# RWKV-7 state pass of a two-layer encoder kernel: the score products alternate between the two heads of a pair, and four unused 512-column products per chunk are added

## The reference

```python
def step(S, inp):
    r_t, w_t, k_t, v_t, a_t, b_t = inp
    sa = jnp.einsum('bhvk,bhk->bhv', S, a_t)
    S = S * w_t[:, :, None, :] + sa[..., None] * b_t[:, :, None, :] + v_t[..., None] * k_t[:, :, None, :]
    return S, jnp.einsum('bhvk,bhk->bhv', S, r_t)
_, y = lax.scan(step, jnp.zeros((bsz, H, Dh, Dh), F32), xs)
```

## Time and profile before

| | us |
|---|---|
| median of 3 runs | 1537.95 |
| lowest and highest | 1529.24 and 1540.2 |
| the profiled execution, its time | 1530.25 |
| its span in the trace | 1528.4 |
| TensorE busy in the span | 1319.8 (86%) |
| VectorE busy in the span | 893.7 (58%) |
| first state block, about | 1214 to 1344 |
| second state block, about | 1345 to 1421 |

### The profile page before, as it was taken

How to read it: one execution, slowest core, us unless ns; L and a number is a source line. 1 busy time by engine, 2 the same in 40 slices (tenths; PEclk the granted TensorE clock), 3 DMA queues, 4 the chain that set the end, 5 groups by cost and what they waited for, 6 DMA issues and landing times. The chain is left out here.

```text
span 1528.4 us, 20526 instructions
## 1 busy us (share of the span) xinstructions
PE 1319.8 (86%) x8434; PEld 1103.1 (72%) x8434; DVE 893.7 (58%) x1191; ACT 480.3 (31%) x822; POOL 307.5 (20%) x156
## 2 busy tenths in 40 slices
PE   4999999899779969959997999998334799999698
PEld 4677888678569848858886888885122698889587
DVE  5277754930257664159975665843888758265841
ACT  5233244222346651132421122312553211212310
POOL 2232211211023362032211111221301300000320
PEclk9999999989889979979999999999665557799899
DMA  5212112320300042232331425221000000010523
GB/s 183 43 42 66 31 46 70 96 70 15 138 22 2 2 138 83 96 76 90 99 97 52 121 64 176 52 83 56 0 1 1 1 1 1 2 56 2 193 82 112
DMA packets 117558, 97.79 MB, mean 64 GB/s; under 512 B 37016, under 2 KB 102680, under 8 KB 117336
## 3 DMA queue, kind: packets, MB, share of 16 engines
q1 hardware_dynamic: 103832, 77.45, 17.1%
q10 hardware_dynamic: 13632, 19.01, 3.8%
HBM read 70.23 MB, written 24.51 MB: 62 GB/s over the span
## 5 line engine op out<-in xcount | busy, mean ns | idle before, releaser
L167 PE MATMUL banks<-xt_lo,w_hi 128*128 128x512 f32 x816 | 323.2, 396 | 6.2 <-POOL w_lo L497 6.2
L168 PE MATMUL banks<-xt_hi,w_lo 128*128 128x512 f32 x816 | 319.9, 392 | 0.0
L169 PE MATMUL banks<-xt_hi,w_hi 128*128 128x512 f32 x816 | 319.6, 392 | 0.0
L497 POOL TENSOR_TENSOR w_lo<-features,w_hi 128x1024 fp32r<-128x1024 f32 x55 | 148.9, 2708 | 529.5 <-ACT w_hi L506 529.5
L167 PEld LDWEIGHTS banks<-xt_lo,w_hi 128*128 128x128 f32 x816 | 154.6, 189 | 42.1 <-POOL w_lo L497 6.7
L169 PEld LDWEIGHTS banks<-xt_hi,w_hi 128*128 128x128 f32 x816 | 154.5, 189 | 32.7
L168 PEld LDWEIGHTS banks<-xt_hi,w_lo 128*128 128x128 f32 x816 | 154.5, 189 | 31.2
L550 ACT ACTIVATE temporaries<-banks 128x1024 f32<-128x1024 f32 x47 | 56.1, 1193 | 328.5 <-PE banks L169 319.8
L506 ACT ACTIVATE w_hi<-features 128x1024 fp32r<-128x1024 f32 x55 | 57.8, 1055 | 27.9 <-PE banks L169 26.7
L295 PE MATMUL banks<-temporaries,features 128*128 128x128 f32 x256 | 38.3, 314 | 27.5 <-DVE temporaries L272 27.5
L167 PE MATMUL banks<-xt_lo,oout_mh 128*128 128x512 f32 x128 | 51.1, 399 | 11.9 <-DVE xt_lo L1581 11.9
(11 more groups left out here) (449 smaller groups left out, 2601.2 us busy)
## 6 DMA issues: line engine op xcount, KB each, us to landing
features<-in_even_w_in SPq DMA_DIRECT2D x26, 512.0 KB, 4.0
features<-in_odd_w_in SPq DMA_DIRECT2D x25, 512.0 KB, 4.3
features<-in_x SPq DMA_DIRECT2D x8, 512.0 KB, 8.6
even_gates<-temporaries ACTq DMA_DIRECT2D x8, 512.0 KB, 2.6
features<-even_gates SPq DMA_DIRECT2D x8, 512.0 KB, 8.1
features<-in_even_w_out SPq DMA_DIRECT2D x8, 512.0 KB, 3.5
temporaries<-in_x SPq DMA_DIRECT2D x8, 512.0 KB, 4.6
h_between_layers<-features SPq DMA_DIRECT2D x8, 512.0 KB, 3.1
```

What stands on the lines that cost most here:

```text
L167: nc.tensor.matmul(out, w[0], x[1], start=start, stop=False)
L168: nc.tensor.matmul(out, w[1], x[0], start=False, stop=False)
L169: return nc.tensor.matmul(out, w[0], x[0], start=False, stop=stop)
L497: nc.gpsimd.tensor_tensor(wl[n % 2], wr[n % NW], wh[n % 2].bitcast(F32), ALU.subtract).then_inc(low, 1)
```

## The change

`pairs` now walks over the three products outside and over the two heads inside, so that neighbouring products use opposite row halves of the array and write different banks. It waits once, for both copies of the previous pair. A new helper `unread` multiplies a broadcast column of `hot_r` with `hot_r` repeated to 512 columns, and nothing reads the result. One such product stands in each `turn`, behind its wait and ahead of its transposes (into the bank of the transposes, which they overwrite), and two stand ahead of the wait for SA in step 5 (into the bank of `read`, which R has left). That is four for each chunk and 64 in the kernel.

```diff
     def tensor(pe):
+        def unread(bank):
+            nc.tensor.matmul(co.ps[:, bank, :].rearrange("p (a b) -> p a b", b=32), co.hot_r[:, 0:1].to_broadcast([P, P]),
+                             co.hot_r.rearrange("p (o b) -> p o b", o=1).to_broadcast([P, 16, 32]), start=True, stop=True)
+
         def turn(c, j):
             if c or j:
                 pe.wait_ge(tok_out, 2 * c + j)
+            unread(2)
             for i, src in enumerate((x.b, x.k, x.v)):
                 last = nc.tensor.transpose(turns[:, i * P:(i + 1) * P], src[:, j, c * P:(c + 1) * P], ident)
             last.then_inc(turned, 1)
 
         def pairs(c, j):
             ct = slice(c * P, (c + 1) * P)
-            for a, rows in enumerate(halves):
-                h = 2 * j + a
-                if c or j:
-                    pe.wait_ge(kept, 4 * c + h - 1)
-                for i, (key, query) in enumerate(((x.b, x.r), (x.k, x.kk), (x.k, x.r))):
-                    last = nc.tensor.matmul(scores(h)[:, i * P:(i + 1) * P], key[rows, j, ct], query[rows, j, ct], start=True, stop=True)
-                last.then_inc(pairs_made, 1)
+            if c or j:
+                pe.wait_ge(kept, 4 * c + 2 * j)
+            for i, (key, query) in enumerate(((x.b, x.r), (x.k, x.kk), (x.k, x.r))):
+                for a, rows in enumerate(halves):
+                    last = nc.tensor.matmul(scores(2 * j + a)[:, i * P:(i + 1) * P], key[rows, j, ct], query[rows, j, ct], start=True, stop=True)
+                    if i == 2:
+                        last.then_inc(pairs_made, 1)
...
             yield 10 * c + 6
+            for _ in range(2):
+                unread(3)
             pe.wait_ge(sa_out, c + 1)
```

## The result

| | us |
|---|---|
| median after (4 runs, 1514.38 to 1517.98) | 1517.18 |
| median before (4 runs, 1529.24 to 1540.2) | 1535.38 |
| ratio after to before, with its 95% interval | 0.9899 (0.986 to 0.9938) |
| profiled execution before and after | 1530.25 and 1514.38 |

A second set of runs of the changed kernel gave 1518.69 and a ratio of 0.9917 (0.9882 to 0.9952). The change saves about 1%. The forecast was 1517, with 20.4 us saved; the ratio stands for 15.5 us, and the two profiled executions differ by 15.9. The 52 executions of the kernel before that stand beside the experiments have a median of 1530.5, and against that the saving is 12 to 13 us.

A forecast was written before the change was run, and what follows sets the result against it. TensorE was taken to bound both state blocks, in the first through its 0.50 clock. First block -26.7, clock falls +5, second block +1.3 summed to -20.4 us, giving 1517 us, with 1504 to 1536 to hold 8 times in 10.

The forecast's parts named there:

- Part 1: Scores in each chunk: alternating halves overlap, saving 0.59 us a block at half clock and 0.33 at full.
- Rival C: TensorE in each chunk: alternation brings no overlap, products cost full price, 19 us slower, 1557 us; chance 0.05.
- The joined wait: Ahead of each block of scores: the single wait for both of VectorE's copies costs nothing in sum.
- Part 2: Unused products in each chunk: none hides in waits; four cost 0.87 us at full clock, 1.70 at half.
- Part 3: First state block: clock rises in the first chunk and mostly stays up, 130.0 to 103.3 us, 26.7 us less.
- the sum: State blocks: -26.7 us for the first, +5 for renewed clock falls, +1.3 for the second, -20.4 us in all.
- two falls: First state block: clock falls again where the array is thin; 2.5 us for each of two, 5 us lost.
- My rule, length times clock: First state block: each chunk's length times granted clock gives its work at full clock, 8.2 to 15.4 us.
- A (the clock stays): First state block: TensorE is already occupied, so the clock stays as it is; +4.5 us, 1542 us; chance 0.16.
- B (VectorE takes over): First state block: clock rises but chunks wait for VectorE, half the gain goes; about -10 us, 1528; chance 0.13.

The follow-up runs named there:

- the run with the thin products: Changed kernel, but each unused product contracts over 32 rows instead of 128, with the same 512 columns: 1563.88 us, ratio 1.0217.
- the late ones alone: Alternating scores, with unused products only in the first state block from the fifth chunk's growth on: 1514.2 us, ratio 0.989.

## Why the prediction was right, and where its reasons were not

**Part 1, the overlap of the alternating scores: right.** I took 0.86 us for a block at full clock, and it took 0.87. The saving is 0.32 us a block, shown by the timeline and by the run with the scores alone. At half clock, for which I had 1.58 us, the run with the thin products has 1.58 (L2411 to L2446):

```profile
1240.78 1.65 PE L2411 MATMUL banks<-features 64*128 64x128 f32 x12
1242.36 1.97 PE L2446 MATMUL banks<-temporaries,big 128*128 128x64 f32 x8
```

Rival C is out. The joined wait cost nothing that the second block's chunks show.

**Part 2, the price of a product: a little low.** I took 0.217 us from stretches in which such products follow each other. Between float32 products one costs 0.25 us on average over a chunk (9.7 against 8.7 us with the scores of before, 9.1 against 8.1 with the new ones). So a chunk at full clock became 0.35 us longer (8.74 to 9.09) and not 0.2. At half clock one ahead of the transposes is 0.59 us and two ahead of the growth are 1.00 (1309.87 to 1310.87 in the changed kernel), for the 0.42 each that I took:

```profile
1323.96 0.79 PE L2394 MATMUL banks<-one_hot 128*128 128x512 f32 x1
...
1324.55 0.84 PE L2402 MATMUL banks<-constants,features 128*128 128x128 f32 x3
```

That none of it hides held. With the block's start at 0.50, the second block lost 4.7 us and not 1.3.

**Part 3, the clock: the sign right, the split wrong.** The step that failed is "I expect the clock to rise in the first chunk and mostly stay up", in its second half. For chunks 1 to 5 the sum had 56.3 us against 71.0, and 52.4 came; the clock was up in the first of them and not midway. For chunks 6 to 8 it had 39.2 us plus 5 for "two falls", and they took 15.6, 20.1 and about 18. My rule, length times clock, took these chunks to run at nearly full clock. But the clock falls there again: 33 us at 0.50 in the 63 us from chunk 6 to the second half's first read, where "two falls" at 2.5 us each stood for 10. That term alone is some 10 us too good. What makes the clock fall there isn't shown. The groups of the inverting program are thin, and TensorE waits for copies between them, but the kernel with the products in the first block has two courses in the same chunks, 62.6 us at 0.74 and 54.2 at 0.87.

Term by term, the sum had -0.2 us for the start, -14.7 for chunks 1 to 5, -6.8 for chunks 6 to 8 with the falls, and +1.3 for the second block. The two profiles have -1.2, -18.6, +5.9 (with the start of the second block) and +4.7. That is 9.2 us less for the state blocks, where the forecast had 20.4. The other 6.8 of the 15.9 us lie in code that the change doesn't touch. The time of 1517 was luck in one more way: it was taken from 1537.95, the median of three runs; from the 1530.5 of the 52 later ones the same 20.4 us would have given 1510.

**What the early gain was worth.** It was credited against one course of the kernel before. Its second profile had the same 52 us with no change at all. What the change really does is to shorten the time at the low clock in sum: some 81 us at 0.50 from first to last read became 40, twice, and 184.4 us came of 192 to 194. That is 8 to 10 us, and 1.2 more at the start of the block.

**What the products are for.** I laid the clock to both parts together, and the prediction treated the products as what fills the chunk. The early clock needs neither both nor the products, and in the kernel before it came up once with neither. The second block, where half of them stand, gives nothing for them. If they are worth something in the first block, it is in the middle stretch: 63.3, 62.6 and 54.2 us with them, 66.0 without, 68.7 with the late ones alone. But these are single profiles of kernels whose own courses differ by 8 us, and the medians don't settle it: 1512.96 and 1513.3 with the first block's products, 1516.39 without any, all intervals overlapping. All of the change's measured saving comes with the alternating scores alone.

**The rivals.** A (the clock stays) did not come. Its reading, that an occupied engine is enough, is refuted twice: by the 51 us of the earlier trace rows in the trace of before, and by the thin products, with which TensorE was at least as occupied and the clock lower. The sentence of the Trainium skill's page "TensorE: Matmul & The Clock Gate" (section "What's actually happening") on how busy the PE has been holds here only if busy is not read as occupied. B (VectorE takes over) came in part: chunk 3 is VectorE's, at 11.4 us, and the waits for its copies are the 3.0 and 1.2 us above. That is not half of the gain of chunks 1 to 5, 18.6 us. The state blocks' balance of 9.2 us is near B's 10, but for other reasons: the low clock of the late chunks and the price of the products.

**What stays open.** The medians say 12.7 to 15.5 us, and the traces show 9 to 11 for the state blocks. The times of before reach from 1521.66 to 1543.45 over all sets, and its three profiled executions lie at 1529 to 1532. Their spread goes with the clock: of the 52, the 17 of 1536 us and more have a mean granted clock of 0.889 to 0.900, the eight under 1525 have 0.903 to 0.909. So longer and shorter courses exist that no profile caught; where in the kernel they differ isn't known. The start of the first block moves by some 4 us between executions of the changed kernel, in code that the change doesn't touch. I didn't separate these. Why the clock takes one course or the other in the same program stays open too. That the close fit of 1517 to 1517.18 is owed to errors that cancel is clear from the terms above.

## What to carry to other kernels

Where an engine's clock depends on what it does, one profile is one course of that clock: profile the kernel before a second time before a slow stretch is credited as a gain, and set the time of each profiled execution beside the median: two of the profiles here lay 11 us off it. Products that contract over half the rows should alternate between the halves, into different banks; here it saved a quarter of the block, and alone it gave as short a time as the whole change. Unused products are a price paid at every place where they stand, so put them, if at all, only where traces show the clock down, and not ahead of steps that form a chain with another engine's copies. A higher granted clock is not yet a shorter time: here they raised the one and left the other.

## What the runs showed of the hardware that was not expected

- One program has two courses of the granted clock with nearly the same sum: 71.0, 57.4 and 64.0 us for its three stretches, or 52.0, 72.7 and 69.4.
- A 512-column float32r product between float32 products costs 0.32 us alone and 0.29 as one of two, against 0.217 in a row of its kind, all at full clock; over 32 of the 128 rows a chunk is 0.2 us longer for each.
- With thin products TensorE was busy for 145 of 150 us, and its clock was at 0.50 for some 119 of them, longer than with no unused products in their place (57).
